# First layer of the sample compression: three output blocks from four products, two samples per pass

## What is computed

```python
def compress_blocks(x, pe, w1, w2):        # x: (8, 1024, 4 heads, 64)
    r = CMP_BLOCK // CMP_STRIDE            # 32 // 16 = 2
    c = x.reshape(B, Tk // CMP_STRIDE, CMP_STRIDE, H, D)
    n_cmp = Tk // CMP_STRIDE - r + 1       # 63
    blocks = jnp.concatenate([c[:, j:j + n_cmp] for j in range(r)], axis=2)
    blocks = blocks + pe[None, None, :, None, :].astype(x.dtype)
    flat = jnp.moveaxis(blocks, 3, 2).reshape(B, n_cmp, H, CMP_BLOCK * D)
    return jax.nn.silu(flat @ w1) @ w2     # w1: 2048 x 256, w2: 256 x 64
```

## Time and profile before

| | |
|---|---|
| runs | 1497.38, 1498.01, 1500.58 us; median 1498.01 |
| profiled execution | 1501.14 us, span 1499.5 us |
| PE busy | 1381.5 us (92%) |
| DVE, ACT, POOL busy | 688.1, 334.1, 212.2 us |
| mean granted TensorE clock | 0.936 of 2.4 GHz |
| DMA | 236.08 MB, mean 157 GB/s |
| first-layer matmuls of the compression (L797) | 1024 records, 228.2 us busy |
| `steps`, until `project_out` begins | 285 to 622.67 us |

### The profile page before, as it was taken

How to read it: one execution, slowest core, us unless ns; L and a number is a source line. 1 busy time by engine, 2 the same in 40 slices (tenths; PEclk the granted TensorE clock), 3 DMA queues, 4 the chain that set the end, 5 groups by cost and what they waited for, 6 DMA issues and landing times.

```text
span 1499.5 us, 25796 instructions
## 1 busy us (share of the span) xinstructions
PE 1381.5 (92%) x10168; PEld 1101.0 (73%) x10168; DVE 688.1 (46%) x1513; ACT 334.1 (22%) x863; POOL 212.2 (14%) x293
## 2 busy tenths in 40 slices
PE   7996898889899999999999999987778879999996
PEld 3454676558687888789999974685545458999996
DVE  1805536531112121056776538617723415677742
ACT  2114434432222221010000001326734311000000
POOL 0102085000000000011111111060012211111100
PEclk9996899969999999999999999957889979999998
DMA  7438697985454541044543634250035664454340
GB/s 253 149 113 295 228 339 244 312 276 169 131 167 164 170 156 57 0 144 138 169 152 116 211 114 150 80 165 11 1 119 187 201 211 139 143 169 151 117 155 32
DMA packets 145642, 236.08 MB, mean 157 GB/s; under 512 B 9554, under 2 KB 101970, under 8 KB 145106
## 3 DMA queue, kind: packets, MB, share of 16 engines
q1 hardware_dynamic: 140386, 212.39, 42.8%
q0 software_dynamic: 5136, 22.05, 4.3%
HBM read 229.09 MB, written 13.64 MB: 162 GB/s over the span
## 4 chain that ended last, share of the span: by engine, by line
PE 83%; DVE 6%; DMA 3%; ACT 3%; SPq 2%; issue 2%; POOL 0%; DVEq 0%; ACTq 0%; POOLq 0%
PE ps L713 18%; PE ps L797 15%; PE ps L508 10%; PE ps L738 10%; PE ps L472 9%; PE ps L681 4%; PE ps L691 2%; PE ps L818 2%; PE ps L925 2%; PE ps L613 2%; PE ps L663 1%; PE ps L514 1%; SPq L361 1%; DMA ring<-in_cache_kv 1%; SPq L464 1%
## 5 line engine op out<-in xcount | busy, mean ns | idle before, releaser
L797 PE MATMUL ps<-big,proj 128*128 128x252 f32 x1024 | 228.2, 380 | 0.0
L797 PEld LDWEIGHTS ps<-big,proj 128*128 128x128 f32 x1024 | 192.8, 192 | 27.3 <-issue 5.0
L1047 ACT ACTIVATE big<-ps 64x256 f32<-64x256 f32 (+3 forms) x300 | 136.2, 467 | 195.8 <-PE ps L472 193.8
L508 PE MATMUL ps<-ring,xT 128*128 128x512 f32 (+1 forms) x384 | 161.0, 575 | 3.4 <-DMA ring<-in_w_in 3.4
L472 PE MATMUL ps<-ct,ring 128*128 128x128 f32 x960 | 144.3, 295 | 18.5 <-DMA ring<-in_cache_kv 5.9
L472 PEld LDWEIGHTS ps<-ct,ring 128*128 128x128 f32 x960 | 112.7, 149 | 60.8 <-issue 31.4
L508 PEld LDWEIGHTS ps<-ring,xT 128*128 128x128 f32 x384 | 70.1, 193 | 81.9 <-issue 78.0
L1683 DVE COPY big<-ps 64x256 f32<-64x256 f32 x128 | 54.1, 422 | 156.1 <-PE ps L472 154.8
L713 PE MATMUL ps<-kT,proj 128*128 128x144 f32 x960 | 124.2, 286 | 0.0
L713 PEld LDWEIGHTS ps<-kT,proj 128*128 128x128 f32 x960 | 120.3, 190 | 0.0
L1878 POOL TENSOR_TENSOR big<-rows 128x576 f32<-128x576 f32 x22 | 51.0, 2318 | 261.4 <-DVE rows L1592 228.1
(11 more groups left out here) (284 smaller groups left out, 2018.2 us busy)
## 6 DMA issues: line engine op xcount, KB each, us to landing
ring<-in_cache_kv SPq DMA_DIRECT2D x128, 512.0 KB, 5.8
ring<-in_w_gu SPq DMA_DIRECT2D x44, 1024.0 KB, 7.6
ring<-in_w_in SPq DMA_DIRECT2D x11, 2048.0 KB, 8.1
ring<-in_w_down SPq DMA_DIRECT2D x16, 1408.0 KB, 6.5
ring<-in_cache_kv SPq DMA_DIRECT2D x64, 256.0 KB, 3.0
ring<-in_w_out SPq DMA_DIRECT2D x4, 2048.0 KB, 8.1
ring<-in_cache_kv SPq DMA_DIRECT2D x64, 128.0 KB, 3.0
ring<-in_state_win SPq DMA_DIRECT2D x16, 512.0 KB, 5.2
```

The costliest lines, as they stand in the source:

```text
L508: last = mm(ps[b + t][:, 0:w], xT[:, k, t * P:(t + 1) * P], src[:, k, :], start=k == 0, stop=k == KD - 1)
L797: last = mm(ps[j % 2][:, 0:NKV * NCS], w1r(j // 2, o)[:, (j % 2) * P:(j % 2 + 1) * P], KC[:, b % 2, (j // 2) * 4:(j // 2) * 4 + 4, o % 8, ...
L1047: return f(out, in_, ACT.Copy)
```

## The change

Let c(n) be chunks. For three neighbouring blocks the kernel now forms four products:

- M0 = A·(c0 - c2), M1 = (A+B)·(c1 + c2), M2 = (A-B)·(c2 - c1) — applied with weights A, A+B, A-B — and M3 = B·(c1 - c3), the numbers of `s` in the code
- 2·y0 = M1 + M2 + 2·M0, 2·y1 = M1 - M2, 2·y2 = M1 + M2 - 2·M3; the factor 0.5 goes into the silu's scale.

63 blocks are 21 groups of three, so a product has 8 matmuls (8 pairs of positions) with 2 samples x 4 heads x 21 = 168 columns, and one column more (pe's own, from which the bias comes) for the first pair of samples. Keys of all four pairs are done first (kp 0 to 3), then the values (kp 4 to 7). `product(i, part)`: i = 0..63, kp = i // 8, output half (i // 4) % 2, product i % 4; part 0 and 1 are four matmuls each. Below, "place a" is i % 8.

PE, core of the diff:

```diff
+        V_AFTER = {0: 3, 3: 4, 6: 5, 9: 6, 12: 7, **{20 + 4 * i: 8 + i for i in range(8)}}
...
+        for n in range(3):
+            value_steps(n)
+        steps += [("turned", 0, g) for g in range(8)]
+        steps.append(("sums", 0))
+        for i in range(64):
+            kp, a = i // 8, i % 8
+            if kp < 7 and a < 4:
+                steps.append(("turned", kp + 1, 2 * a))
+            if a == 3 and kp >= 1:
+                steps.append(("second", kp - 1))
+            steps.append(("product", i, 0))
+            if kp < 7 and a < 4:
+                steps.append(("turned", kp + 1, 2 * a + 1))
+            steps.append(("product", i, 1))
+            if 13 <= i < 19:
+                steps.append(("weights", i - 13))
+            if i in V_AFTER:
+                value_steps(V_AFTER[i])
...
+            def turn_cmp(kp, g):
...
+                if 8 * kp + g >= 1:
+                    pe.wait_ge(k_a[1], 8 * kp + g)
+                    pe.wait_ge(k_d[1], 8 * kp + g)
+                for r in range(4):
+                    a = (b2 * NPG + half * 4 + r) * KVW + i2 * P
+                    last = turn(ps[6][:, r * P:(r + 1) * P], cmp_src[0][:, a:a + P])
...
+            def product(i, part):
...
+                    if i == 32:
+                        pe.wait_ge(s_w1, 64)
...
+                    if si == 0 and u >= 2:
+                        pe.wait_ge(c_y, u - 1)
+                    if hf == 0:
+                        pe.wait_ge(c_x, 4 * kp + si + 1)
+                for o in range(4 * part, 4 * part + 4):
+                    last = mm(cmp_out(u, si, n), w1s(s, o)[:, hf * P:(hf + 1) * P], XS[(4 * kp + si) % XB][:, o, 0:n],
+                              start=o == 0, stop=o == 7)
```

All transposes go through one bank, ps6; its lower 64 partitions are kept by ACT and the upper 64 by DVE (two copies each). DVE then forms the sums of the data, combines the products and forms the sums of the weights; ACT brings three of four products out of PSUM:

```diff
+            def sum_chunks(kp, si):
...
+                for b2 in range(2):
+                    x = [KR[b2][:, :, c:c + 3 * NG - 2:3, :].rearrange("p h m o -> p o h m") for c in range(4)]
+                    a, b, op = ((x[0], x[2], ALU.subtract), (x[1], x[2], ALU.add), (x[2], x[1], ALU.subtract), (x[1], x[3], ALU.subtract))[s]
+                    last = tt(X[:, :, b2 * 84:b2 * 84 + 84].rearrange("p o (h m) -> p o h m", h=NKV), a, b, op)
...
+            def sum_w1(k):
+                A, B = proj[:, 0, 0:8 * CH], proj[:, 1, 0:8 * CH]
+                dve.wait_ge(s_w1, 32 * (k + 1))
+                dve.wait_ge(c_h, 32 * k)
+                tt(proj[:, 2, 0:8 * CH], A, B, ALU.add).then_inc(c_b, 1)
+                tt(proj[:, 0, 8 * CH:12 * CH], A[:, 0:4 * CH], B[:, 0:4 * CH], ALU.subtract)
+                tt(proj[:, 1, 8 * CH:12 * CH], A[:, 4 * CH:8 * CH], B[:, 4 * CH:8 * CH], ALU.subtract).then_inc(c_b, 1)
...
+            def combine(u):
+                dve.wait_ge(c_a, u + 1)
...
+                link(tt(s, t, m3, ALU.add))
+                tt(yc[:, 0:n, 1], t, m3, ALU.subtract)
+                last = tt(yc[:, 0:n, 0], s, twice[:, 0, 0:n], ALU.add)
...
+                tt(yc[:, 0:n, 2], s, twice[:, 1, 0:n], ALU.subtract).then_inc(c_y, 1)
...
+            def double(u):
+                act.wait_ge(c_h, 4 * (u + 1))
...
+                f(twice[:, 0, 0:n], cmp_out(u, 0, n), ACT.Copy, scale=2.0)
+                f(twice[:, 1, 0:n], cmp_out(u, 1, n), ACT.Copy, scale=2.0)
+                copy(half_sum[0][:, 0:n], cmp_out(u, 2, n)).then_inc(c_a, 1)
...
+                elif step[0] == "product" and step[2] == 1:
+                    i = step[1]
+                    kp, a = i // 8, i % 8
+                    if a % 4 == 3:
+                        combine(i // 4)
+                    if i == 31:
+                        sum_w1(1)
+                    if kp < 7 and 3 <= a < 7:
+                        sum_chunks(kp + 1, a - 3)
```

In DVE's program `sum_w1(0)` stands in the keys' stage, between `keep_k0(12, 14)` and `keep_k0(14, 16)`. The silu covers 504 columns now (`silu_cmp`, at places 0 and 4, one unit late). Only one half of w1 is in `proj` at a time, and `cmp` slots hold 2 samples x 8 pages of 128 KB; SP issues the first sample's, POOL the second's:

```diff
-            if cc in (2, 3):
-                plan.append((("w1r", cc - 2), None, 0))
+            if cc == 2:
+                plan.append((("w1r", 0), None, 0))
...
+                        sp.wait_ge(c_h, 30)
+                    for t in range(2):
+                        sp.dma_start(proj[:, t, 0:8 * CH].rearrange("p (i n) -> p i n", n=CH),
+                                     w1_h[:, name[1], 8 * t:8 * t + 8, :]).then_inc(s_w1, 16)
...
+                pool.wait_ge(freed, value)
+                for dst, (c, b, pg, part) in page_jobs_cmp(ring[:, i % SLOTS, :], name[1], 1):
+                    pool.dma_start(dst, c[page(pool, b, pg), :, part, :].rearrange("g s n -> (g s) n")).then_inc(s_half[i % SLOTS], 16)
```

More of the change, by code:

```diff
@@ L282, in trunk @@
+        steps.append(("second", 7))
         steps.append(("back", 3))
+        at = {s: n for n, s in enumerate(steps)}
+        freed_at = []
         for step in steps:
             if step[0] == "v":
-                plan.append((("v0", step[1], step[2]), v_c[0], 4 * step[1] + step[2] + 1))
-            elif step[0] == "c" and step[1] % 8 == 0 and step[1] // 8 < NB:
-                plan.append((("cmp", step[1] // 8), k_p[1], step[1] + 8))
+                entry, when = (("v0", step[1], step[2]), v_c[0], 4 * step[1] + step[2] + 1), at[step]
+            elif step[0] == "turned" and step[2] == 0:
+                entry, when = (("cmp", step[1]), k_p[1], 8 * (step[1] + 1)), at[("turned", step[1], 7)]
+            else:
+                continue
+            if len(freed_at) >= SLOTS and freed_at[-SLOTS] > at[("product", 29, 1)] and (("w1r", 1), None, 0) not in plan:
+                plan.append((("w1r", 1), None, 0))
+            plan.append(entry)
+            freed_at.append(when)
@@ L449, in _ @@
                 elif kind == "cmp":
-                    c = cache_kv1[0].rearrange("g s (two kv) h d -> g s two (kv h d)", two=2)
-                    jobs = [(slot[:, r * 512:(r + 1) * 512], (c, name[1], r, 0)) for r in range(NPG)]
+                    jobs = page_jobs_cmp(slot, name[1], 0)
                 elif kind in ("k1", "v1"):
@@ L739, in down @@
                     last.then_inc(d_p[l], 1)
[L741 to L752, removed]
@@ new lines, in turn_cmp @@
+            def turn_cmp(kp, g):
+                b2, i2, half = g // 4, g // 2 % 2, g % 2
+                if g == 0:
+                    cmp_src[0] = take(pe, "cmp", kp)
+                if 8 * kp + g >= 1:
[4 more added lines that the diff above has]
+                    last = turn(ps[6][:, r * P:(r + 1) * P], cmp_src[0][:, a:a + P])
+                last.then_inc(k_p[1], 1)
@@ new lines, in keep_cmp @@
+            def keep_cmp(kp, g):
+                b2, i2, half = g // 4, g // 2 % 2, g % 2
+                dve.wait_ge(k_p[1], 8 * kp + g + 1)
+                if kp >= 1 and g % 4 == 0:
+                    dve.wait_ge(c_x, 4 * kp)
+                x = ps[6][64:128, :].rearrange("p (n o r) -> p n o r", o=8, r=2)
+                for par in range(2):
+                    last = v.tensor_copy(KR[b2][par * 64:par * 64 + 64, 2 * i2 + 1, 32 * half:32 * half + 32, :], x[:, :, :, par])
+                last.then_inc(k_d[1], 1)
@@ L1695, in prompt1, with keep_second @@
+            def keep_second(kp):
+                dve.wait_ge(c_w, kp + 1)
+                for b2 in range(2):
+                    b = 2 * (kp % 4) + b2
+                    if kp < 4:
+                        last = v.tensor_copy(kc[:, b, :, :], ps[7][:, b2 * P:b2 * P + 2 * NCS].rearrange("p (i n) -> p i n", i=2))
+                    else:
+                        last = v.tensor_copy(vc[0:NCS, b, :], ps[7][0:NCS, b2 * KVW:(b2 + 1) * KVW])
+                last.then_inc(c_we, 1)
             def prompt1():
@@ L1825, in _ @@
                     pick(0, step[1])
-                elif step[0] == "c":
-                    compress(step[1])
+                elif step[0] == "turned":
+                    keep_cmp(*step[1:])
+                elif step[0] == "sums":
+                    for si in range(4):
+                        sum_chunks(0, si)
+                elif step[0] == "second":
+                    keep_second(step[1])
+                elif step[0] == "product" and step[2] == 1:
+                    i = step[1]
[6 more added lines that the diff above has]
+                        sum_chunks(kp + 1, a - 3)
             project_out(0)
```

280 lines of the change are left out of this document (130 added, 150 removed).

## The result

| | before | changed |
|---|---|---|
| runs, median | 1498.84 us (1497.38 to 1500.58) | **1490.06 us** (1488.09 to 1492.05) |
| profiled execution, span | 1501.14, 1499.5 | 1491.82, 1490.2 |
| PE busy | 1381.5 (92%) | 1316.0 (88%) |
| `project_out` begins | 622.67 | 612.83 |

The ratio is 0.9942, with a 95% interval of 0.9919 to 0.9965: the kernel is faster by 8.8 us, 0.6%, where 40 were forecast, and the time lies outside the range of 1441 to 1482. PE lost its work: 65 us of busy time are gone. The end did not follow. From `project_out` on, both kernels take the same (1490.2 - 612.83 = 877.4 us, before 1499.5 - 622.67 = 876.8), so the whole difference lies ahead of it.

What follows compares the result with a forecast made beforehand. PE alone was taken to set the pace in `steps`; 324.3 us start, 216.8 work and 41.7 waits put `project_out` at 582.8, 39.9 earlier, so median 1458 us. Own range 1449 to 1470, with rivals 1441 to 1482.

Steps and rivals of the forecast that it cites:

- The start: Start of `steps`: eight serial transpose groups 16.6 us, four pairs of sums 7.0, copies 0.9; PE resumes at 324.3 us.
- Bounds: Limits on a 672-element sum's price: no less than 0.70 us, upwards 1.4 to 1.5, with 0.75 taken.
- clock terms of 2.0 and 2.6: PE's clock needs time to rise: 2.0 us after the start, 2.6 after the wait for w1's second half.
- Products: First-layer matmuls in `steps`: 168 columns take 142.5 ns a record, 2.28 us a product; 71.7 us less.
- Starts of a kp: PE waits while DVE combines before keeping the new group: 1.7 us each at six starts, 10.2 us.
- Loads: PE waits for page loads of `cmp` and value slots: 3.0 us for later ones, 2.0 for `cmp2`.
- Second half of w1: First product of kp 4: PE waits 13 us for the load, 3.4 behind DVE, clock's rise 2.6; 17.3 in all.
- Rival 2: Sums at 1.5 us: DVE's eight overrun at six starts, 14.4 us; start 6, weights' sums twice 4.5; 1487 us, chance 0.08.
- Rival 4: DVE becomes the bound: gain gone at 1.85 us a sum; at 2.3 us slower than before, 1523 us; chance 0.04.
- Rival 3: `cmp` slots' page halves come late, POOL's issues held up by DVE's sums: six times 4.3 us, 1484 us; chance 0.12.
- Rival 1: Waits close: w1's second half comes while PE has products, or value slots free SP sooner; 17 us vanish, 1441; chance 0.13.
- Rival 5: Weight loads at 190 ns, not columns, set the products' pace: 194.6 us, kernel 1507 us, slower; chance 0.02.

Runs made afterwards that it cites:

- e3: Changed kernel with kept data laid out as head, position, chunk, so sums read with a step of 3 elements instead of 24; 1471.14 us, ratio 0.9823.
- e11: Changed kernel with one edit: VectorE keeps the new group of transposes before it combines the last place's four products; 1477.38 us, ratio 0.9855.
- e6: e3 with the new group also kept before the products are combined, w1 loaded where the change has it; 1463.48 us, ratio 0.9768.
- e8: e3 with each `cmp` slot from the fourth on loading 8 of its 16 page pieces, the rest keeping old data; 1459.54 us, ratio 0.9747.
- e10: Changed kernel without the second load of w1, its wait and its sums, so values run with the keys' weights; 1472.4 us, ratio 0.9839.
- e4: Changed kernel with the load of w1's second half right behind cmp5 in SP's order, ahead of v11 and v12; 1482.16 us, ratio 0.9883.
- the best version: Changed kernel with three edits: e3's layout, w1's second half loaded earlier, new group kept before the combining; 1451.02 us, ratio 0.9685.

## Why the prediction was wrong, by its steps

**The step that failed** is the price in "The start": "between 512 in 573 ns and 1024 in 1271 I take 0.75 us", and its upper bound of 1.4 to 1.5 under "Bounds". A sum took 1.70. Both ends came from rows of operations whose reads are neighbours; the access pattern, a step of 24 elements, was named there as unseen and then priced by rows without it. The prediction asked for a row that is near in size, and the near row had to be near in pattern. Even for neighbours 0.75 was low: 852 ns were measured. The 573 ns were misread, too: they are a mean over shapes ("+3 forms"), and nine of the 21 operations in it have 256 elements. Those of 128 x 512 alone cost 691 ns, by shape in the kernel before:

```profile
L1410 DVE TENSOR_TENSOR proj<-proj,gr 128x512 f32<-128x512 f32 x8 | 5.5, 691 | 0.3
```

Between 691 and 1271 an estimate for 672 elements is 0.87 us, close to what neighbours cost.

**Where the 30 us are** by which `project_out` came later than forecast (612.8 against 582.8): PE resumed at 329.2 instead of 324.3, 4.9 us. From there on the waits are 48.4 us (those of the trace without the 8.1 that ended at 329.2) instead of 37.1 (the forecast's 41.7 without its clock terms of 2.0 and 2.6): 11.3. The rest of that stretch, PE at work, is 283.6 - 48.4 = 235.2 us instead of 216.8 + 4.6: 13.8. Laid start to start in PE's timeline, about 11 us of the 235.2 are what half clock added (seven half products 7.9, three groups of transposes 1.3, two value steps 1.6), 6.4 more than the 4.6 that were allowed. Almost 7 more are the products at full clock: 151.6 us instead of 144.8.

How much of it is the sum's price, `e3` shows: with 1.10 us a sum, `project_out` begins at 595.1, so 17.7 of the 30 are VectorE's. The other 12.3, reckoned in the same way in `e3`, are 3.4 of waits (270.6 us from 324.4 on, 40.5 of them waits) and 8.7 of PE's work. Of the 8.7 again some 7 are the products at full clock (151.9 us instead of 144.8), and 1.7 is half clock beyond the 4.6 (6.3 in all: three half products, two groups of transposes, and one value step behind a wait, which took 3.62 us where 1.92 is usual). The price of a product came from 16 and more records in a row. Where half a product stands between two groups of transposes it takes 1.21 us, in the changed kernel from 339.85 to 341.06, and not 1.14; there are near 50 of them at full clock, which is an estimated 3.4 of the 7 us.

Point by point, with rows of PE's timeline of the changed kernel, at the start and the end of `steps`:

```profile
318.57 2.59 PE L829 MATMUL ps<-big,proj 128*128 128x169 f32 x8 [2.36 <-DVE big L1742]
329.24 1.09 PE L504 MATMUL ps<-ct,ring 128*128 128x128 f32 x4 [8.09 <-DVE kT L1724]
...
339.85 1.31 PE L829 MATMUL ps<-big,proj 128*128 128x169 f32 x8
341.06 0.63 PE L504 MATMUL ps<-ct,ring 128*128 128x128 f32 x4
...
595.14 11.67 PE L829 MATMUL ps<-big,proj 128*128 128x168 f32 x80
609.62 2.05 PE L790 MATMUL ps<-w,big 128*63 128x64 f32 x32 [2.82 <-ACT big L1267]
```

- *Products.* Right in the mechanism, 7 us too good in size. At full clock 80 records, five products, took 11.67 us, 2.33 each or 146 ns a record (forecast 2.28), and halves take 1.21. So some 65 us were saved instead of 71.7, and PE's busy time fell by 65 us.
- *Start.* The eight serial rounds are right (2.14 us a round against 2.07; first product at 318.57, forecast near 320). The four pairs are 3.2 us each instead of 1.75 (from 315.08 to 327.94). The first slot landed 1.8 us earlier than the point that was to stay.
- *Starts of a kp.* 1.7 us each were forecast. The mechanism (combine ahead of the keep) was right, and `e11` and `e6` show it by taking it away. Its size was off twice: VectorE came from its sums without a gap, and the six starts waited for 1.84, 4.16, 4.40, 2.96, 3.16 and 2.59 us; and the half clock behind the wait, some 1.5 us, was counted at the first start and at w1 alone.
- *Loads.* 5.0 were forecast; the changed kernel shows 5.3 for late `cmp` slots and 1.2 for value slots. In faster kernels they grow (`e3`: 6.2, 4.3 and 0.3), and `e8` gives 11.6 us back, w1's queue included. Mechanism right, size nearly (6.5 for 5.0).
- *Second half of w1.* Right: 17.3 forecast, 17.7 by `e10`; a wait of 13 forecast, 15.5 measured. It could be avoided almost by half with one line of `plan` (`e4`).
- *Picking of heads.* 3.0 us forecast for three or four starts; three such groups waited 1.13, 1.05 and 1.07.
- *End.* The last silu made 2.82 us of wait, and 0.9 for `project_out`, as forecast.

**The rivals.** Rival 2, slow sums whose eight overrun the time between the two combines, is what happened, with a chance of 0.08 and 1487 at 1.5 us a sum. Its second term did not come: the sums of the weights, whose reads are neighbours, took 4.6 us (479.85 to the keep at 484.44) where the forecast had 4.8. Rival 4 is the same mechanism at a price that makes the kernel slower than before, held at 0.04 because "the largest price in the rows is 2.04 ns an element"; it was 2.54. Its formula gives 8 x 0.95 + 6 x 4.0 = 31.6 at 1.70 us and so 1489.7, close to 1490.06, but that is in part luck: from 1.70 to 1.10 us it takes off 28.8 where `e3` gained 18.9, and it holds 2.8 at 1.10 where 13 us were missing. It was too steep by the 10 us that the other terms were short. The range ended at 1482, below the prediction's own rivals 2 (1487) and 3 (1484), 0.20 together; with rivals 4 and 5 that leaves out 0.26, not "less than 2 in 10".

Rival 3 (page halves held up by VectorE's sums) did not happen. POOL's issues start 1.15 us apart whether VectorE copies (at 339) or sums without a gap (at 385):

```profile
338.90 0.55 POOL L2010 DMA_DIRECT2D ring<-in_cache_kv  x1 [0.60 <-issue]
340.05 0.55 POOL L2010 DMA_DIRECT2D ring<-in_cache_kv  x1 [0.60 <-issue]
...
384.75 0.55 POOL L2010 DMA_DIRECT2D ring<-in_cache_kv  x1 [0.60 <-issue]
385.90 0.55 POOL L2010 DMA_DIRECT2D ring<-in_cache_kv  x1 [0.61 <-issue]
```

Nor does POOL make a sum dear: from 315.08 on, where POOL issues nothing until 337.75, sums take 1.64 to 1.70 us as elsewhere. Rival 1, 1441, assumed that the waits close; the one wait that it named can be closed in the largest part, and the best version comes within 10 us of it. Rival 5 (weight loads) is refuted by 146 ns a record.

## What to carry to other kernels

When work moves from a full engine to an idle one, price it there by a row with the same access pattern, or give both ends a wide bound; here the pattern of the reads made 852 ns into 1705, and the part of it that another layout takes away was worth 18 us of what PE had saved. Ask for such a row by its shape, since a mean over shapes fits none of them. Then lay the receiving engine's instructions between two hand-overs end to end: if they fill the time, whatever stands ahead of the copy that the other waits for is on the path, and its order is worth more than its length (12.7 us for moving four short operations, and once the sums of the weights). And each wait that puts the clock down has to be counted with the work behind it, not once but at every place.

## What the runs showed of the hardware

- VectorE's fp32 operation with two inputs and 672 elements per partition: 852 ns with a step of 1 element in SBUF, 855 with 2, 1095 with 3, 1392 with 8, 1705 with 24; with one input at 1 and the other at 24, 1668. Steps 3, 8 and 24 were read in runs of 21 elements, steps 1 and 2 without a break. The Trainium skill ("SBUF — State Buffer", Door 1: The DMA port swizzle, the note on cachelines) has lines of 16 bytes, of which an access that crosses to a new one pays a penalty, and says that fp32 can stride by 4 for free. The runs agree that reads which each fall on a new line cost more (1392 and 1705 against 852). The note has no size for the penalty: from 8 to 24, where each read is on a new line either way, it still grows by 0.31 us. Whether a step of 3 is free they don't show, since its 29% may in part be the runs of 21.
- After a wait of 4.16 us four transposes took 1.08 us and half a product 2.28, the half clock (1.2 GHz); in `e3` the same start waited for 1.37 us and they took 0.63 and 1.31, at the full 2.4. So 2.8 us of waiting for VectorE cost 4.2 there.
- GpSimd's DMA issues start 1.15 us apart beside VectorE's two-input sums as without them, and the sums take 1.64 to 1.70 us where GpSimd issues nothing.
